# The index stage's value and weight projections, computed with the activations as the stationary operand instead of computed feature-major and transposed

## The reference, cut to what matters

```python
h = x @ w_in                       # x: 512 positions x 1024 features
v = h[..., o2:o3]                  # 128 columns: the values, one head for all 16 query heads
qi = apply_partial_rope(...)       # 8 index heads of 64
ki = apply_partial_rope(...)       # index key, 64
wi = h[..., o6:]                   # 8 columns: one weight for each index head
rel = relu(einsum('bthd,bsd->bths', qi_b, ki))
score = einsum('bths,bth->bts', rel, wi_b) * INDEX_SCALE
_, idx = lax.top_k(score, topk)    # 128 keys for each query, then attention over them
```

## Time and profile before

| | |
|---|---|
| median of 3 runs | 1848.44 us |
| the profiled execution | 1847.91 us |
| its span (first to last instruction) | 1846.1 us |
| PE busy | 1746.0 us (95%) |
| PE's weight loads busy | 1437.8 us (78%) |
| matmuls and weight loads | 7994 each |
| DVE busy | 1100.5 us (60%) |
| POOL busy | 1011.5 us (55%) |
| ACT busy | 618.7 us (34%) |
| mean granted clock of TensorE | 0.976 |

### The profile page before, as it was taken

How to read it: one execution, slowest core, us unless ns; L and a number is a source line. 1 busy time by engine, 2 the same in 40 slices (tenths; PEclk the granted TensorE clock), 3 DMA queues, 4 the chain that set the end, 5 groups by cost and what they waited for, 6 DMA issues and landing times. The chain is left out here.

```text
span 1846.1 us, 22799 instructions
## 1 busy us (share of the span) xinstructions
PE 1746.0 (95%) x7994; PEld 1437.8 (78%) x7994; DVE 1100.5 (60%) x1673; ACT 618.7 (34%) x1153; POOL 1011.5 (55%) x564
## 2 busy tenths in 40 slices
PE   7799999988999999976999999999998999999999
PEld 5688788766887888855778888888786888887887
DVE  6877633357552454478678746546577956775234
ACT  4355411133221222022534332332433117765123
POOL 5555466654667666644654646555463563333554
PEclk9999999988999999988999999999998999999999
DMA  5222223221233222321322222222231222111222
GB/s 194 74 81 80 80 92 101 92 80 57 91 101 98 97 97 96 102 69 57 103 80 69 80 80 84 78 90 69 79 104 57 80 93 67 48 57 46 91 80 80
DMA packets 47954, 155.03 MB, mean 84 GB/s; under 512 B 6912, under 2 KB 7040, under 8 KB 47744
## 3 DMA queue, kind: packets, MB, share of 16 engines
q1 hardware_dynamic: 47008, 152.35, 25.3%
q10 hardware_dynamic: 864, 1.57, 0.2%
HBM read 151.80 MB, written 2.10 MB: 83 GB/s over the span
## 5 line engine op out<-in xcount | busy, mean ns | idle before, releaser
L632 POOL TENSOR_SCALAR w_hi<-raw 128x1024 fp32r<-128x1024 f32 (+1 forms) x280 | 311.2, 1111 | 799.3 <-issue 561.0
L634 POOL TENSOR_TENSOR w_lo<-raw,w_hi 128x1024 fp32r<-128x1024 f32 (+1 forms) x280 | 700.2, 2501 | 23.4
L658 PE MATMUL bank<-op_hi,w_hi 128*128 128x512 f32 x1080 | 433.9, 402 | 45.0 <-DVE op_lo L2105 15.9
L660 PE MATMUL bank<-op_hi,w_lo 128*128 128x512 f32 x1080 | 425.4, 394 | 0.0
L659 PE MATMUL bank<-op_lo,w_hi 128*128 128x512 f32 x1080 | 425.2, 394 | 0.0
L658 PE MATMUL bank<-r,w_hi 128*128 128x512 f32 (+1 forms) x872 | 348.4, 400 | 10.8 <-DVE r L2096 6.4
L660 PE MATMUL bank<-r,w_lo 128*128 128x512 f32 (+1 forms) x872 | 342.2, 392 | 0.0
L659 PE MATMUL bank<-r,w_hi 128*128 128x512 f32 (+1 forms) x872 | 342.1, 392 | 0.0
L658 PEld LDWEIGHTS bank<-op_hi,w_hi 128*128 128x128 f32 x1080 | 206.2, 191 | 96.3 <-issue 32.0
L660 PEld LDWEIGHTS bank<-op_hi,w_lo 128*128 128x128 f32 x1080 | 205.4, 190 | 44.0
L659 PEld LDWEIGHTS bank<-op_lo,w_hi 128*128 128x128 f32 x1080 | 206.3, 191 | 41.6 <-issue 1.2
(11 more groups left out here) (239 smaller groups left out, 2257.5 us busy)
## 6 DMA issues: line engine op xcount, KB each, us to landing
raw<-in_weights SPq DMA_DIRECT2D x278, 512.0 KB, 3.6
h<-in_x SPq DMA_DIRECT2D x4, 512.0 KB, 8.1
out<-h SPq DMA_DIRECT2D x8, 256.0 KB, 2.0
cst<-in_consts SPq DMA_DIRECT2D x1, 1156.5 KB, 10.4
rope_cos<-in_p ACTq DMA_DIRECT2D x3, 256.0 KB, 3.8
rope_sin<-in_p ACTq DMA_DIRECT2D x3, 256.0 KB, 4.3
rope_cos<-in_positions SPq DMA_DIRECT2D x2, 256.0 KB, 11.4
raw<-in_weights SPq DMA_DIRECT2D x4, 128.0 KB, 2.4
```

What stands on the lines that cost most here:

```text
L632: pool.tensor_scalar(hi, raw[:, r, 0:w], 1.0, 0.0, ALU.mult, ALU.add).then_inc(hi_ready, 1)
L634: pool.tensor_tensor(lo, raw[:, r, 0:w], hi.bitcast(F32), ALU.subtract).then_inc(split_ready, 1)
L658: pe.matmul(o, ah, bh, start=start, stop=False, skip_group_check=skip)
L660: return pe.matmul(o, al, bh, start=False, stop=stop, skip_group_check=skip)
```

## The change

Units 6 and 7 are computed with the roles exchanged. The activations (128 features by 128 positions) are the stationary operand and the weights the moving one, 128 columns for the values and 8 for the index weights. The result has the positions on its partitions at once: for each of the four blocks of 128 positions, 8 blocks of features with three matmuls each go into that block's columns of bank 2 or bank 3. The transposes `turn_v` and `turn_w` and the copies `vf` and `wf` are gone. `vh` reads bank 2, `vl` bank 2, and `wi` bank 3 with the scale.

```diff
-        idx_act = [..., "kh", "vf", "wf", "vh", "wi"]
+        idx_act = [..., "kh", "vh", "wi"]
...
-              ["turn_v"] + [f"s{q}{x}" for q, x in pairs[:2]] + ["turn_w"] + [f"s{q}{x}" for q, x in pairs[2:]])
+              [f"s{q}{x}" for q, x in pairs])
...
-        value_rows, weight_rows = fx[:, 2, :], fx[0:IH, 1, :]
...
-            pe.wait_ge(split_ready, u + 7)
-            blocks(ps[2][:, :], (u + 6) % 2, [(k, k) for k in range(KD)], x2_hi, x2_lo).then_inc(unit_done, 1)
-            c = u + 7
-            pe.wait_ge(split_ready, c + 1)
-            for k in range(KD):
-                mm = split_mm(ps[3][0:IH, :], w_hi[:, c % 2, k, 0:IH], w_lo[:, c % 2, k, 0:IH], x2_hi[:, k], x2_lo[:, k], k == 0, k == KD - 1)
-            mm.then_inc(unit_done, 1)
-            pe.wait_ge(a.sem, a.at("vf"))
-            for t in range(QT):
-                mm = pe.transpose(ps[6][:, t * P:(t + 1) * P], value_rows[:, t * P:(t + 1) * P], ident)
-            z.done(mm, "turn_v")
+            for n, (name, width) in enumerate((("v", P), ("wi", IH))):
+                c = u + 6 + n
+                pe.wait_ge(split_ready, c + 1)
+                for t in range(QT):
+                    for k in range(KD):
+                        mm = split_mm(ps[2 + n][:, t * width:(t + 1) * width], x2_hi[:, k, t * P:(t + 1) * P],
+                                      x2_lo[:, k, t * P:(t + 1) * P], w_hi[:, c % 2, k, 0:width], w_lo[:, c % 2, k, 0:width],
+                                      k == 0, k == KD - 1)
+                mm.then_inc(unit_done, 1)
             pe.wait_ge(d.sem, d.at("kil1"))
             n = 0
             for q in range(1, QT):
                 for x in range(IH):
-                    if n == 2:
-                        pe.wait_ge(a.sem, a.at("wf"))
-                        for t in range(QT):
-                            mm = pe.transpose(ps[7][:, t * IH:(t + 1) * IH], weight_rows[:, t * P:(t + 1) * P], ident[0:IH, 0:IH])
-                        z.done(mm, "turn_w")
...
             act.wait_ge(unit_done, u + 7)
-            hi(a, "vf", value_rows, ps[2][:, :])
+            hi(a, "vh", dv_hi[:, 0], ps[2][:, :])
             act.wait_ge(unit_done, u + 8)
-            a.done(act.activation(weight_rows, ps[3][0:IH, :], ACT.Copy, scale=INDEX_SCALE), "wf")
-            act.wait_ge(z.sem, z.at("turn_v"))
-            hi(a, "vh", dv_hi[:, 0], ps[6][:, :])
-            act.wait_ge(z.sem, z.at("turn_w"))
-            hi(a, "wi", st[:, 0:QT * IH], ps[7][:, 0:QT * IH])
+            a.done(act.activation(st[:, 0:QT * IH], ps[3][:, 0:QT * IH], ACT.Copy, scale=INDEX_SCALE), "wi")
...
-            lo(d, "vl", dv_lo[:, 0], ps[6][:, :], dv_hi[:, 0])
+            lo(d, "vl", dv_lo[:, 0], ps[2][:, :], dv_hi[:, 0])
```

More of the change, by code:

```diff
@@ L464, in build @@
         ple_stage("ple2", True)
-        idx_act = ["qf0", "qf1", "hi0", "qf2", "hi1", "qf3", "hi2", "qf4", "hi3", "qf5", "kih0", "kih1", "kh", "vf", "wf", "vh", "wi"]
+        idx_act = ["qf0", "qf1", "hi0", "qf2", "hi1", "qf3", "hi2", "qf4", "hi3", "qf5", "kih0", "kih1", "kh", "vh", "wi"]
         idx_dve = [f"zero{n}" for n in range(4)]
```

## The result

| | before | changed |
|---|---|---|
| median | 1848.68 us (4 runs, 1847.91 to 1849.13) | 1864.34 us (4 runs, 1862.50 to 1865.72) |
| the profiled execution | 1847.91 us | 1865.39 us |
| its span | 1846.1 us | 1863.6 us |
| PE busy, matmuls | 1746.0 us, 7994 | 1769.7 us, 8130 |
| mean granted clock | 0.976 | 0.970 |

The change made the kernel slower by 15.7 us, a ratio of 1.0085 (95% interval 1.0067 to 1.0102). Forecast were 1859 us, within 1850 to 1864: the right sign and in the main the right mechanism, and 5 us too little.

What follows compares the result with a forecast made beforehand. PE's work plus holes was taken to bound the kernel, the index stage alone deciding. Third score 8.6 us later, POOL collision 1.3 and late clock 0.5 gave 10.4; 1847.91 + 10.4 + 0.5 = 1858.8, so 1859 us, range 1850 to 1864.

Steps and rivals of the forecast that it cites:

- What bounds the kernel: Whole kernel: PE's work plus its holes; what the index scores gain or lose goes one for one to the end.
- the budget of 8.4 us: Unit 7's end to third score: removing hole, transposes and two ACT copies gives at most 9.9 - 1.5 = 8.4 us.
- The prediction's 9.9 us more for the two units: Units 6 and 7: 192 matmuls at full-clock rates take 20.7 us, against 10.9 us for the present 48.
- 192 matmuls paced by their loads: Units 6 and 7: stationary loads set the pace, 0.112 us per matmul at 128 columns, 0.104 at one column.
- The rival with cheaper loads: Units 6 and 7: a repeated load of the same tile costs nothing, 13.7 us for both, 1844.5 us total; 3%.
- The clock falls in unit 7: Unit 7: its 96 matmuls of 8 columns lose the full clock, so it takes 17.3 us (16.3 to 18.3).
- The rival in which it holds: Unit 7: clock stays at 1.00, unit 7 takes 10.0 us, scores run warm, 1849.5 us total; 15%.
- the one in which it falls in unit 6: Unit 6: clock already falls in its 128-column matmuls and unit 7 runs cold, +10 us on top, 1869; 5%.
- When it falls: Unit 7: clock falls after 3.0 us (2.1 to 3.9), with 29 matmuls at full clock and 67 at half.
- The collision with POOL and the clock's late return: Scores: POOL's split delays DVE's first sums, 1.3 us (0 to 2.1); warm-up ends later, 0.5 us (0 to 2).
- The sum for the stage: Index stage: 8.6 + 1.3 + 0.5 = 10.4 us slower, with bounds 6.8 to 14.6.

Runs made afterwards that it cites:

- x1_wide: The changed kernel with unit 7 streaming all 128 columns of its weight tile (120 zero padding) instead of 8: 1853.74 us, 1.0023 of before.
- x6_late_split: The changed kernel with POOL's split of the second query projection's unit held back until after the last index score: 1860.59 us, 1.0062 of before.
- x3_weights: The kernel before with unit 7 alone changed (activations stationary for the index weights), unit 6 as before: 1854.42 us, 1.0036 of before.
- a_again: The changed kernel run once more, not altered: 1862.37 us, 1.0075 of before.

## Why the prediction was half right

- *What bounds the kernel, and the budget of 8.4 us:* right. The hole went, and the stage's gain or loss passed to the end one for one; behind the first projection the four profiles of the two programs differ by less than 0.2 us. (The prediction's 9.9 us more for the two units should read 9.8: 20.7 - 10.9.)
- *192 matmuls paced by their loads:* right. Forecast were 0.112 us at 128 columns and 0.104 at 8, measured 0.111 and 0.11. Unit 6 took 10.7 us, forecast 10.8. The rival with cheaper loads falls; so does, for this case, the Trainium skill's 81 ns for such a pair (TensorE: Matmul & The Clock Gate, Back-to-back issue gap).
- *The clock falls in unit 7:* right, and shown by x1_wide. The rival in which it holds and the one in which it falls in unit 6 (1.00 through it in five profiles) both fall.
- *When it falls: this is the step that failed.* "It fell 2.1 us after the last wide matmul there, and in the hole 3.9 us after it [...]. The middle is 3.0 us." It fell 1.0, 0.9 and 1.0 us into unit 7 in the changed kernel's two profiles and in x6_late_split, and 2.8 in x3_weights, where unit 6 stays wide. With 9 matmuls at full clock instead of 29 unit 7 took 19.5 us where I had 17.3 and at most 18.3. Both of my samples hold idle time of PE behind the wide matmuls, and neither is a long row of narrow ones, so they gave no bounds for this row. What sets the moment stays open: three profiles agree within 0.2 us, and the one with another unit 6 in front differs.
- *The collision with POOL and the clock's late return:* forecast 1.3 + 0.5 us, measured 18.8 - 16.7 = 2.1 from the third score to the first projection, and x6_late_split gave all of it back. I had it act on the two-input sums alone; the one-input sum stood still too, 2.45 us.
- *The sum for the stage:* forecast 10.4, measured 12.8 and 12.9. Of the 2.4 us too little, 2.2 are unit 7's.
- *Left out altogether: the chance ahead of the stage.* The first three runs of before lay within 1 us of each other, and I took that for the kernel's spread. It is about 6 us over 17 runs. The sum had no term for it. This is the second step that failed, and the larger part of the miss: the stage's 12.8 us lie within the sum's own bounds (6.8 to 14.6) and would have given 1861, inside the range. The other 3 us or so are chance, and with them the median lies 0.3 us outside. On which side of so near a bound four runs fall is luck: those of a_again have a median of 1862.37.

## What to carry to other kernels

When a transpose is traded for swapped operands, count the loads of the stationary operand, not the columns: here the 24 loads of a unit became 96, and a matmul of 8 columns cost as much as one of 128. A row of very narrow matmuls can also lose the clock while the engine is never idle, and the work behind it then starts slow. And before computing anything differently to close a hole, look at what order alone can put into it, and at what each earlier end will release: here a helper engine's split, started at the wrong moment, took back 3.9 us of a gain of 9 by the profiles, and 6.0 of 8.6 by the medians.

## What the runs showed of the hardware

- TensorE, issuing back to back, kept 2.4 GHz through 96 matmuls of 128 moving columns (10.7 us) and through 192 in x1_wide (21.4 us), and lost it 0.9 to 1.0 us (three profiles) and 2.8 us (x3_weights) into a row of 96 with 8 columns, which had the same loads.
- A matmul of 8 columns with its load of 128x128 takes 0.11 us at the full clock and 0.213 at half of it.
- DVE's first sum, with one input tile, took 2.45 us beside POOL's two-input split and 0.35 alone; a two-input instruction took 2.81 beside it and 0.68 alone.
- One unaltered kernel varied by 5.8 us (1846.95 to 1852.74) over 17 runs. In two profiles of it the same instruction stood 3.1 us apart at 1400 us.
